# Router logits of two mixture-of-experts layers: the router's weights stationary, 256 tokens moving, and two transposes back

## The reference, cut to what matters

```python
def hier_moe(h, w_rg, b_rg, w_re, b_re, w_gate, w_up, w_down):
    xt = h.reshape(t, d)                                   # 256 x 1024, after RMSNorm
    g_logits = xt @ w_rg + b_rg                            # 4 groups
    g_sel = jnp.argmax(g_logits, axis=-1)                  # one group for each token
    ...
    e_all = (xt @ w_re + b_re).reshape(t, N_GROUPS, EXPERTS_PER_GROUP)   # 4 x 8 experts
    e_logits = jnp.take_along_axis(e_all, g_sel[:, None, None], axis=1)[:, 0]
    top_p, top_j = lax.top_k(jax.nn.softmax(e_logits, axis=-1), TOP_K)   # two experts
    ...
    return expert_dispatch(xt, eid, gate, w_gate, w_up, w_down)          # SwiGLU, 1024 -> 512 -> 1024
```

## Time and profile before

| what | value |
| --- | --- |
| median of 3 runs | 1398.35 us |
| lowest and highest run | 1394.01 and 1401.41 us |
| span of the profiled execution (first to last instruction) | 1394.9 us |
| mean granted TensorE clock over the span | 0.866 of full speed |
| TensorE matmul busy | 1021.8 us (73%) |
| TensorE weight load busy | 747.5 us (54%) |
| VectorE, ScalarE, GpSimd busy | 324.3, 284.5, 40.5 us |
| data moved | 458.52 MB, mean 329 GB/s |

### The profile page before, as it was taken

One profiled execution on the slowest core, in us unless ns is written; L12 is line 12 of the kernel. 1 busy time (PEld: TensorE's weight loads), 2 busy tenths in 40 slices (PEclk: granted clock), 3 DMA queues, 4 the chain that ended last, 5 costly groups with the idle time before them and its releaser, 6 DMA issues.

```text
span 1394.9 us, 29191 instructions
## 1 busy us (share of the span) xinstructions
PE 1021.8 (73%) x12868; PEld 747.5 (54%) x12868; DVE 324.3 (23%) x665; ACT 284.5 (20%) x615; POOL 40.5 (3%) x74
## 2 busy tenths in 40 slices
PE   5978977757767666675799999887675666756675
PEld 2945666535445443553577778665454544534353
DVE  4356241111101001110644545421110011101011
ACT  3443221101101000110553443511101000101002
POOL 2013200000000000000000000000000000000000
PEclk9985789999879897888799999988988988879687
DMA  9630069999999999999746634469999999999994
GB/s 317 239 121 0 1 244 401 421 420 421 420 418 420 420 421 418 420 422 394 258 144 229 226 130 176 162 255 421 415 421 419 419 420 420 420 419 420 422 419 195
DMA packets 79753, 458.52 MB, mean 329 GB/s; under 512 B 4960, under 2 KB 14240, under 8 KB 63120
## 3 DMA queue, kind: packets, MB, share of 16 engines
q1 hardware_dynamic: 78512, 452.96, 80.0%
q0 software_dynamic: 1120, 3.68, 0.9%
HBM read 455.58 MB, written 1.05 MB: 327 GB/s over the span
## 4 chain that ended last, share of the span: by engine, by line
PE 45%; DMA 39%; SPq 6%; issue 4%; DVE 3%; ACT 1%; POOL 1%; DVEq 0%; PEldq 0%; POOLq 0%; ACTq 0%
DMA ring<-in_w_down 20%; DMA ring<-in_w_up 11%; DMA ring<-in_w_gate 7%; PE wk L949 7%; SPq L457 6%; PE wk L976 4%; PE wk L637 4%; PE wk L639 4%; PE wk L638 4%; PE wk L933 4%; PE acc L917 2%; PE wk L624 2%; PE acc L637 2%; PE acc L639 2%; PE acc L638 1%
## 5 line engine op out<-in xcount | busy, mean ns | idle before, releaser
L949 PE MATMUL wk<-ring,arena 128*32 128x128 f32 x8192 | 299.7, 308 | 158.2 <-DMA ring<-in_w_up 79.8
L949 PEld LDWEIGHTS wk<-ring,arena 128*32 128x32 f32 x8192 | 257.7, 124 | 208.7 <-DMA ring<-in_w_up 91.9
L976 PE MATMUL wk<-ring,arena 128*32 128x256 f32 x2048 | 168.6, 483 | 70.9 <-DMA ring<-in_w_down 56.0
L976 PEld LDWEIGHTS wk<-ring,arena 128*32 128x32 f32 x2048 | 76.8, 134 | 139.7 <-issue 122.5
L1648 DVE TENSOR_TENSOR arena<-wk,arena 128x128 f32<-128x128 f32 x64 | 18.7, 292 | 433.9 <-ACT arena L1283 433.9
L1656 DVE COPY arena<-wk 32x256 f32<-32x256 f32 x128 | 54.3, 424 | 264.8 <-PE wk L976 263.9
L1283 ACT ACTIVATE arena<-wk 128x128 f32<-128x128 f32 x64 | 17.7, 277 | 450.1 <-PE wk L949 450.1
L1435 DVE TENSOR_TENSOR slot_parts<-ring,slot_parts 128x1024 fp32r<-128x1024 f32 (+1 forms) x78 | 97.2, 1301 | 31.7 <-ACT slot_parts L1142 31.2
L1294 ACT ACTIVATE arena<-wk 32x256 f32<-32x256 f32 x128 | 47.7, 373 | 225.4 <-PE wk L976 224.7
L1142 ACT ACTIVATE slot_parts<-ring 128x1024 fp32r<-128x1024 f32 (+1 forms) x78 | 81.8, 1114 | 48.9 <-PEq L1074 23.2
L933 PE MATMUL wk<-arena,xn 128*128 128x128 f32 x512 | 71.1, 305 | 27.7 <-issue 18.3
(11 more groups left out here) (269 smaller groups left out, 1089.1 us busy)
## 6 DMA issues: line engine op xcount, KB each, us to landing
ring<-in_w_gate SPq DMA_DIRECT2D x64, 2048.0 KB, 35.9
ring<-in_w_up SPq DMA_DIRECT2D x64, 2048.0 KB, 30.7
ring<-in_w_down SPq DMA_DIRECT2D x64, 2048.0 KB, 34.2
ring<-in_w_in_o SPq DMA_DIRECT2D x8, 2048.0 KB, 9.1
ring<-in_w_in_o SPq DMA_DIRECT2D x8, 1024.0 KB, 12.0
ring<-in_w_out_o SPq DMA_DIRECT2D x4, 2048.0 KB, 7.7
ring<-in_w_in_e SPq DMA_DIRECT2D x3, 2048.0 KB, 18.4
ring<-in_w_out_e SPq DMA_DIRECT2D x2, 2048.0 KB, 12.1
```

The source lines that it names most:

```text
L949: last = nc.tensor.matmul(wk[0][32 * j:32 * j + 32, part * P:(part + 1) * P], xe[:, k, :], w_[:, k, j * P:(j + 1) * P], start=(k == 0), st ...
L976: last = nc.tensor.matmul(wk[3][32 * j:32 * j + 32, 0:256], hidT[:, k, :], wd[:, k, j * 256:(j + 1) * 256], start=(k == 0), stop=(k == 3))
```

## The change

The roles of the two operands of the router's product are exchanged. The weights of the router (36 columns) become the stationary operand and all 256 tokens the moving one, so that the logits come out transposed, 36 partitions by 256 tokens, in `wk[0]`. ScalarE copies them to SBUF (into `gT`'s place, under the name `lgT`). TensorE turns them back in two transposes into `wk[1]`, where VectorE reads them. There is one new step on TensorE's list and one on ScalarE's, both called `lgT`.

```diff
+        lgT = gT
...
-        router_pe = lambda l: [f"lg{l}", f"rk{l}"]
+        router_pe = lambda l: [f"lgT{l}", f"lg{l}", f"rk{l}"]
...
-        router_act = lambda l: [f"ge{l}", f"ee{l}"]
+        router_act = lambda l: [f"lgT{l}", f"ge{l}", f"ee{l}"]
...
                 for c in range(TC):
                     normed(e_, c)
-                    last = project(wk[0][:, c * 64:c * 64 + NR], lambda k: xnT[:, k, tok(c)], lambda k: wr[:, l, k, :])
+                project(wk[0][0:NR, 0:SEQ], lambda k: wr[:, l, k, :], lambda k: xnT[:, k, :]
+                        ).then_inc(pe_s, PE.done(f"lgT{l}"))
+                pe.wait_ge(act_s, A.at(f"lgT{l}"))
+                for c in range(TC):
+                    last = nc.tensor.transpose(wk[1][:, c * 64:c * 64 + NR], lgT[0:NR, tok(c)], ident[0:NR, 0:NR])
                 last.then_inc(pe_s, PE.done(f"lg{l}"))
 
                 seed_wide()
...
                 drain_xT(f"ffn{l}")
+                act.wait_ge(pe_s, PE.at(f"lgT{l}"))
+                nc.scalar.activation(lgT[0:NR, :], wk[0][0:NR, 0:SEQ], ACT.Copy).then_inc(act_s, A.done(f"lgT{l}"))
                 act.wait_ge(dve_s, V.at(f"gd{l}"))
...
                 dve.wait_ge(pe_s, PE.at(f"lg{l}"))
-                logits = wk[0][:, 0:128].rearrange("p (c n) -> p c n", c=TC)[:, :, 0:NR]
+                logits = wk[1][:, 0:128].rearrange("p (c n) -> p c n", c=TC)[:, :, 0:NR]
```

## The result

| kernel | median | lowest to highest | runs |
| --- | --- | --- | --- |
| before | 1397.63 us | 1390.34 to 1401.41 | 20 |
| changed | 1400.95 us | 1397.35 to 1403.52 | 20 |

The ratio is 1.0028, 95% interval 1.0017 to 1.0040: the changed kernel is slower by 0.28%, some 3.9 us (2.4 to 5.6); the two medians are 3.3 us apart. The forecast was +0.56 us, with 1393.8 to 1403.8 as the range. The time lies in the range and the sign is that of the forecast; the size is not. The measured loss is seven times the one predicted.

What follows compares the result with a forecast made beforehand. The router's chain ahead of each layer's first weight order was taken as the bound. Per layer +0.38 us to VectorE and -0.1 for the seeds gave +0.56 in all: 1398.35 + 0.56 = 1398.9 us, range 1393.8 to 1403.8.

Steps and rivals of the forecast that it cites:

- What bounds the kernel: Both layers: the router's chain of waits sets the first weight order; a later order costs layer 0 its full delay.
- What can be told from no change: Whole kernel: a measurement can't tell less than about 0.5% (7 us) from no change.
- The wait for chunk 1: Ahead of the router's product: TensorE must wait for both chunks' copies, +0.77 us, not less than 0.72.
- The product: Router's product: 16 records of 256 moving columns, 5.06 us plus 0.2 for start and end; range 3.6 to 7.2.
- the forecast case: Router's product: clock goes from 0.50 to 1.00 within it, 5 us long; +0.56 us in all, chance 0.52.
- rival 2: Router's product: clock stays at half throughout, 7.2 us; layer's balance +2.42, time 1403.2 us; chance 0.15.
- The copy: After the product: one ScalarE copy of 36 x 256 from PSUM, 0.38 us plus 0.04 signal, no table load.
- The two transposes: After the copy, on TensorE: 0.60 us including 0.14 signal, ends 0.4 and 0.9; then 0.04 to VectorE.
- The seeds: Behind the transposes: 3.6 us at full clock, off the chain; ranks start 4.83 after VectorE; -0.1 us per layer.
- After the ranks: From the ranks on, gather included: nothing changes in kind; gather now 5.40 us, no change taken.
- a sign of being wrong: Gather: the prediction is wrong if its time moves by more than a microsecond.
- The change does what it says: Router's product: rival 5 denied this, the product still bound by its weight load; chance within 0.04 for things unseen.

Runs made afterwards that it cites:

- the wait alone: Kernel before, with chunk 0's router product made to wait for the copies of chunk 1 too; ratio 1.0010 (0.9999 to 1.0022).
- split seeds: Kernel before, with chunk 0's two seeds moved between the two chunks' transposes and chunk 1's two behind the ranks; ratio 0.9954 (0.9935 to 0.9973).

## Why the prediction was half right

- *What bounds the kernel*: right for this change. The chain of the router sets the first order, and the sum of the two stretches (+4.5 and +3.1 us in two pairs of profiles) goes with that of the runs (+3.9). With the wait alone such a sum was far above what the runs said, so this agreement is in part luck.
- *What can be told from no change*: the prediction took 0.5% as the least. With 20 runs of each kernel, 0.28% stands clear of 1.
- *The wait for chunk 1*: +0.77 predicted; the start moved by 0.86 in the profile, 0.88 alone on the kernel before. "That is its whole price" was too low: with the wait alone VectorE starts 1.2 us later, mostly because the old product had also begun 0.2 us before the end of the transposes.
- *The product*: 5.06 + 0.2 predicted; 5.56 and 6.50 measured, 5.54 and 6.00 in the second profile. This is the term that was mis-sized ahead of VectorE. The clock did go from half to full inside the product, as in the forecast case, but later than in the seeds that stood model for it: at a mean of 0.65 and 0.55, with rival 2's half clock nearly reached in layer 1. Rival 2's own price, 7.2, is somewhat too high: at the half clock the records start 0.43 us apart, which for 16 makes an estimated 6.8 us.
- *The copy*: 0.38 predicted, 0.38 measured, no table load. *The two transposes*: 0.60 and 0.04 with signals; from the end of the copy (197.46 + 0.39 = 197.85) to VectorE's start (198.24) 0.39 measured. The 0.14 for the signal to TensorE is shown by no row and was 0.04 here. Copy and way back together 0.78.
- *The seeds*: 3.6 predicted, 3.70 measured, and off the chain; the ranks start 4.82 and 4.83 after VectorE's start as said.
- *After the ranks*: "I take no change" is the step that failed. The gather takes 0.8 and 1.3 us more, and 0.7 and 1.1 more in the second pair. In layer 1 that is over the microsecond which the prediction itself named as a sign of being wrong. That it is the clock is shown: 0.60 in the gather here, and 1.00 with 3.57 us when dense work stands right ahead. What shifts it is not shown. For the seeds' earlier end speaks that the gather was 6.68 and 5.77 in the kernel before with half its seeds moved away and nothing else. Against it speak the gathers of 5.62 and 5.89 with half the seeds moved away in the changed kernel, 5.49 and 5.31 with the product by chunk as well, and 6.19 with the wait alone, where the seeds still reach the ranks.

On the average of the two pairs of profiles, the gather makes 2 x 1.0 us, and "to VectorE" is 2 x 0.5 us above the +0.38 predicted for it. With the +0.56 of the forecast that is an estimated +3.5, within the interval of the measured +3.9. Both errors went the same way. The forecast time still lies near the measured one because both errors are small beside the kernel, and the range held because it is 10 us wide; the sum that gave +0.56 was not borne out.

The change does what it says, and as it stands it doesn't pay. The prediction took the half clock of the old product as given and asked what the new one would do. The two seeds moved forward show that the clock was the matter: the old product falls from 6.67 to 3.51 us with them, the new one from 5.56 and 6.50 to 3.6. At the same clock the two products cost about the same. The old one loads 128 columns 32 times, 0.208 us each at half clock and 0.110 (3.51 / 32) at full; the new one moves 256 columns 16 times, 0.43 at half (its weight loads start 0.43 apart) and 0.23 at full. Both come to 4096 columns: the work was only carried from the loads to the streams, and the wait, the copy and the way back came on top. What the exchange can still bring is a clock that rises sooner. By chunk, without the wait, its product took 4.35 and 5.00 us where the 36-column records took 6.67, and that kernel was faster than before (0.9983). With two seeds ahead of either product that advantage is gone.

The Trainium skill (TensorE: Matmul & The Clock Gate, LDWEIGHTS) gives P / 1.2 ns for a weight load of P columns, an estimated 107 ns for 128. The trace agrees at the full clock, with 110 ns per record, and not at the half clock, where a record takes 208 ns.

## What to carry to other kernels

Before the operands of a small product are exchanged, look at the granted clock in its stretch: a chain of short matmuls after idle time may run at half speed, and moving work that has to be done anyway into that idle time nearly doubled its speed here, for no new operation. Count both forms at the same clock, in loads times stationary columns and in records times moving columns, before counting what the exchange adds. And when work is moved off the chain, read the clock of the stage behind it again: here the gather, whose own instructions are the same in every version, took between 3.57 and 6.76 us. Last, check whether the stage is still what the kernel waits for once it is shorter.

## What the runs showed that was not expected

- A float32 weight load of 128 columns follows the granted clock, as streaming does: 0.208 us a record at 0.50, 0.110 at 1.00.
- Thirty-two records that move only 36 columns each ran at clock 1.00 for their 3.51 us in layer 0 once two seeds had brought it up, and stood at 0.50 for 6.67 us when nothing had. They didn't always keep it: in layer 1 of the kernel before with split seeds it fell a microsecond before their end.
- The same exchanged product took 5.55 and 6.49 us in whole, and 4.41 and 5.06 in halves of 128 columns that started 0.9 us sooner, though it takes 3.6 us in either form at the full clock. The sooner rise of the clock within the product (1.1 and 1.4 us) was worth more here than the wait that was removed (0.9 us).
